# Two MLP projections of a streaming encoder step as seven block products in place of eight

## What is computed

```
h = rmsnorm(x, norm_mlp[i])
x = x + jnp.square(jax.nn.relu(h @ mlp_w_up[i])) @ mlp_w_down[i]
```

## Time and profile before

| | us |
|---|---|
| median of 3 runs | 2936.48 |
| lowest and highest | 2935.74, 2940.26 |
| span of the profiled execution | 2935.5 |
| TensorE busy in that span | 2839.6 |
| DVE, ACT, POOL busy | 1153.9, 946.4, 622.9 |

### The profile page before, as it was taken

The page is one execution under the profiler, slowest core; times in us unless marked ns, Lnnn a source line. Parts: engine busy times, 40 slices in busy tenths (PEclk is TensorE's granted clock), DMA queues, the critical chain, the costliest instruction groups (busy, mean ns, idle before and its releaser), DMA issues. The chain is left out here.

```text
span 2935.5 us, 41843 instructions
## 1 busy us (share of the span) xinstructions
PE 2839.6 (97%) x16003; PEld 2508.1 (85%) x16003; DVE 1153.9 (39%) x1778; ACT 946.4 (32%) x1927; POOL 622.9 (21%) x482
## 2 busy tenths in 40 slices
PE   7989997899999999999899999998999999999998
PEld 6878896788998899889798877776899899989997
DVE  5666663343332233223411008886443233323333
ACT  4344444221221122113222229996132112112212
POOL 3100002021211121112121116664031122112211
PEclk9999999999999999999999999999999999999999
DMA  4211113410111011011134448655021011101111
GB/s 141 84 59 44 43 52 97 156 36 29 58 50 36 29 57 50 23 42 58 65 126 152 146 124 196 148 143 168 1 65 44 29 43 57 43 29 43 57 33 75
DMA packets 190619, 214.97 MB, mean 73 GB/s; under 512 B 17312, under 2 KB 151968, under 8 KB 190496
## 3 DMA queue, kind: packets, MB, share of 16 engines
q1 hardware_dynamic: 190496, 213.30, 24.2%
HBM read 165.65 MB, written 47.61 MB: 73 GB/s over the span
## 5 line engine op out<-in xcount | busy, mean ns | idle before, releaser
L1576 DVE TENSOR_TENSOR x<-m_ps,x 128x512 f32<-128x512 f32 x324 | 223.9, 691 | 606.2 <-PE m_ps L76 606.2
L1621 DVE TENSOR_TENSOR m_sq<-m_relu 128x384 f32<-128x384 f32 x192 | 170.8, 890 | 504.9 <-ACT m_relu L1508 504.9
L1508 ACT ACTIVATE m_relu<-m_ps 128x384 f32<-128x384 f32 x192 | 94.5, 492 | 507.5 <-PE m_ps L76 507.5
L74 PE MATMUL m_ps<-h_h,m_up0h 128*128 128x384 f32 x768 | 257.0, 335 | 0.0
L76 PE MATMUL m_ps<-h_h,m_up0l 128*128 128x384 f32 x768 | 256.7, 334 | 0.0
L75 PE MATMUL m_ps<-h_l,m_up0h 128*128 128x384 f32 x768 | 256.7, 334 | 0.0
L74 PE MATMUL m_ps<-h_h,m_up1h 128*128 128x384 f32 x768 | 256.5, 334 | 0.0
L75 PE MATMUL m_ps<-h_l,m_up1h 128*128 128x384 f32 x768 | 256.5, 334 | 0.0
L76 PE MATMUL m_ps<-h_h,m_up1l 128*128 128x384 f32 x768 | 256.5, 334 | 0.0
L1503 ACT CAST m_dn0h<-m_dn_raw 128x1024 fp32r<-128x1024 f32 x16 | 16.8, 1053 | 546.7 <-PE m_ps L76 546.6
L1556 POOL TENSOR_TENSOR m_dn0l<-m_dn_raw,m_dn0h 128x1024 fp32r<-128x1024 f32 x16 | 38.2, 2390 | 527.7 <-ACT m_dn0h L1503 527.7
(11 more groups left out here) (573 smaller groups left out, 7177.8 us busy)
## 6 DMA issues: line engine op xcount, KB each, us to landing
m_up_raw<-in_mlp_w_up SPq DMA_DIRECT2D x64, 512.0 KB, 4.7
m_dn_raw<-in_mlp_w_down SPq DMA_DIRECT2D x64, 512.0 KB, 3.4
h_raw<-scratch_oT SPq DMA_DIRECT2D x4, 1536.0 KB, 15.2
scratch_qr<-a_qrst SPq DMA_DIRECT2D x9, 512.0 KB, 3.4
a_x<-in_x_prompt SPq DMA_DIRECT2D x8, 512.0 KB, 4.9
b_qr<-scratch_qr SPq DMA_DIRECT2D x4, 1024.0 KB, 6.8
scratch_oT<-b_o SPq DMA_DIRECT2D x32, 128.0 KB, 1.7
x<-in_x_prompt SPq DMA_DIRECT2D x4, 1024.0 KB, 13.6
```

The costliest lines, as they stand in the source:

```text
L74: pe.matmul(out, w[0], m[0], start=start, stop=False)
L1508: act.activation(relu[n % 2][:], up_bank(n, first), ACT.Relu).then_inc(relu_done.sem, 1)
L1576: dve.tensor_tensor(x[:, t, cols], bank[:, 4 + n % 3, :], x[:, t, cols], ALU.add).then_inc(added.sem, 1)
L1621: dve.tensor_tensor(sq[n % 2][:], relu[n % 2][:], relu[n % 2][:], ALU.mult).then_inc(sq_done.sem, 1)
```

## The change

The core of the diff:

```diff
+        tok_slot = dict(A11=0, S2=1, S3=2, S1=3, A12=0, S4=1, A22=2)
+        wt_slot = dict(B11=0, T2=1, T3=2, T1=3, B21=1, B22=2, B12=3)
...
+        NORM_ORDER = (0, 1, 2, 3, 8, 4, 5, 6, 7)
...
+        def down_bank(c, n, hp):
+            return 2 * ((14 * c + PAIR_HALF[n] + hp) % 3)
...
+            for c in range(CHUNKS):
+                more = c + 1 < CHUNKS
+                token_hi(c, "S3")
+                token_hi(c, "A12")
+                weight_hi(c, "B21")
+                token_hi(c, "S4")
+                weight_hi(c, "B22")
+                token_hi(c, "A22")
+                weight_hi(c, "B12")
+                weight_hi(c, "T4")
+                if more:
+                    token_hi(c + 1, "S1")
+                    token_hi(c + 1, "A11")
+                    weight_hi(c + 1, "B11")
+                    token_hi(c + 1, "S2")
+                    weight_hi(c + 1, "T2")
+                    weight_hi(c + 1, "T1")
+                    token_hi(c + 1, "u8")
+                    weight_hi(c + 1, "T3")
...
+                if i >= 2 and final:
+                    act.wait_ge(y_out[i % 2].sem, 16 * (i // 2))
+                elif i >= 2:
+                    act.wait_ge(turned_2.sem, 2 * (i - 1))
...
+            def third_sum(c):
+
+                raw = wt_raw[c % 2]
+                pool.wait_ge(*weight_in(c, "22"))
+                if c:
+                    pool.wait_ge(down.sem, down_at(c - 1, "s1"))
+                else:
+                    pool.wait_ge(prod.sem, 9 * PAIRS_FF)
...
+            for c in range(CHUNKS):
+                fourth_sum(c)
+                weight_lo(c, "B21")
+                if c == CHUNKS - 1:
+                    pool.wait_ge(summed.sem, down_at(c, "P1"))
+                    for hp in range(2):
+                        out = total["P2"][:, 2 * hp:2 * hp + 2, :]
+                        pool.tensor_tensor(out, out, total["P1"][:, 2 * hp:2 * hp + 2, :], ALU.add).then_inc(
+                            join_pool.sem, 1)
...
+                dve.tensor_tensor(out, src, out, ALU.add).then_inc(summed.sem, 1)
...
+                token_sum(c, "S3")
+                token_lo(c, "S3")
+                for hp in range(2):
+                    accumulate(c, "P1", hp)
+                token_lo(c, "A12")
+                for hp in range(2):
+                    accumulate(c, "P6", hp)
+                token_sum(c, "S4")
+                token_lo(c, "S4")
                 if last:
...
+                    join_totals("P6", "P1", [(summed, down_at(c, "P6"))])
+                for hp in range(2):
+                    accumulate(c, "P7", hp)
+                token_lo(c, "A22")
+                if last:
+                    join_totals("P3", "P6", [(join_2, 2)])
+                    join_totals("P7", "P6", [(summed, down_at(c, "P7"))])
+                for hp in range(2):
+                    accumulate(c, "P5", hp)
...
+                    token_sum(c + 1, "S1")
+                for hp in range(2):
+                    accumulate(c, "P2", hp)
+                accumulate_sample(c, 0)
+                if not last:
+                    token_lo(c + 1, "A11")
+                    token_lo(c + 1, "S1")
+                    token_sum(c + 1, "S2")
...
+                    token_lo(c + 1, "S2")
+                    weight_sums(c + 1)
+                    token_lo(c + 1, "u8")
+                    for hp in range(2):
+                        accumulate(c, "P4", hp)
...
+                up_product(p, "P1", alpha, "A11", "B11", True)
...
+                pe.wait_ge(parted.sem, 3 * p + 1)
+                up_product(p, "P6", alpha, "S2", "T2", False)
+                after(pe, joined, 3 * (p - 2) + 3)
+                up_product(p, "P5", delta, "S1", "T1", True)
+                pe.wait_ge(parted.sem, 3 * p + 2)
...
+                up_sample(p, 0)
+                up_sample(p, 1)
...
+                pe.wait_ge(parted.sem, 3 * p + 3)
+                up_product(p, "P4", alpha, "A22", "T4", False)
+                pe.wait_ge(joined.sem, 3 * p + 2)
+                up_product(p, "P3", delta, "S4", "B22", False)
...
+                after(pe, summed, down_emptied(c, n, hp))
+                pe.wait_ge(tok_lo[a].sem, c + 1)
+                pe.wait_ge(wt_lo[b].sem, c + 1)
+                for i in range(2):
+                    t = 2 * hp + i
+                    for j in range(2):
+                        last = product(pe, bank[:, down_bank(c, n, hp) + i, :],
+                                       [u[:, j, t * P:(t + 1) * P] for u in tok_op[a]],
+                                       [w[:, j, :] for w in wt_op[b]], j == 0, j == 1)
...
+                for n, a, b in (("P1", "A11", "B11"), ("P6", "S2", "T2"), ("P7", "S3", "T3"), ("P5", "S1", "T1"),
+                                ("P2", "A12", "B21")):
+                    for hp in range(2):
+                        down_product(c, n, hp, a, b)
+                down_sample(c, 0)
+                for hp in range(2):
+                    down_product(c, "P3", hp, "S4", "B22")
+                down_sample(c, 1)
+                down_product(c, "P4", 0, "A22", "T4")
+                if last_chunk and not final:
+                    next_turn(0)
+                    next_turn(1)
+                down_product(c, "P4", 1, "A22", "T4")
```

More of the change, by code:

```diff
@@ new lines, in output_and_mlp_stage @@
+        w_o_parts = made + [parts for parts, _ in w_o_t[len(made):]]
+        w_o_raw = loaded + [raw[:] for _, raw in w_o_t[len(loaded):]]
+        gain = place("gain", [P, D_MODEL], r_at)
+        xn = [place(f"xn{u}", [P, D_MODEL], r_at + 4 * KIB * (u + 1)) for u in range(2)]
+        sum_2 = place("sum2", [P, QUARTER, P], r_at + 12 * KIB)
+        stat = place("stat", [P, NT, 3], r_at + 34 * KIB)
+        stat_2 = place("stat2", [P, NT, 3], r_at + 34 * KIB + 128)
+        half = place("half", [P, 1], r_at + 34 * KIB + 256)
@@ L1361, in output_and_mlp_stage @@
-        added = signal("add", 3)
-        def chunks(engine, body):
-            body(0, False, True)
-            with engine.Fori(1, CHUNKS - 1) as c:
-                body(c, False, False)
-            body(CHUNKS - 1, True, False)
-        def up_bank(n, first):
-            return bank[:, (7, 4)[n] if first and n < 2 else (n + 2) % 4, 0:GROUP]
+        out_done, added = signal("out"), signal("add")
+        x_out = [signal(f"xout{t}") for t in range(NT)]
+        squared, mean, rs, normed, turned, half_set = (signal(n) for n in ("sq", "mean", "rs", "xn", "xt", "half"))
@@ new lines, in up_product @@
+            def up_product(p, kind, out, a, b, start):
+                pe.wait_ge(up_lo.sem, up_at(a, p))
+                if b in ("T2", "T3", "T4"):
+                    out = out.rearrange("p (q c) -> p q c", c=P)
+                for k in range(4):
+                    last = product(pe, out, [w[:, k, :] for w in up[a]], [features(b, k, s) for s in range(2)],
+                                   start and k == 0, k == 3,
+                                   not start)
+                last.then_inc(prod.sem, 1)
@@ new lines, in up_sample @@
+            def up_sample(p, j):
+                out = up_banks(p)[3][:, j * P:(j + 1) * P]
+                for i, n in enumerate((("A11", "A12"), ("A21", "A22"))[j]):
+                    pe.wait_ge(up_lo.sem, up_at(n, p))
+                    for k in range(4):
+                        last = product(pe, out, [w[:, k, :] for w in up[n]], [y[:, 4 * i + k, :] for y in h8],
+                                       i == 0 and k == 0, i == 1 and k == 3)
+                last.then_inc(prod.sem, 1)
@@ L1701, in sb_operands @@
+            if not final:
+                for i in range(2, NT):
+                    next_turn(i)
+    return [piece[:] for piece in ahead]
 def sb_operands(nc, ctx, name):
```

1161 lines of the change are left out of this document (850 added, 311 removed).

## The result

| | before | after |
|---|---|---|
| median, us | 2936.11 | 3003.11 |
| lowest and highest of 4 runs | 2934.92, 2940.26 | 2999.34, 3004.56 |
| span of the profiled execution | 2935.5 | 3002.5 |
| ratio, with 95% interval | | 1.0224, 1.021 to 1.0239 |

What follows compares the result with a forecast made beforehand. The prediction took TensorE, busy 97% of the span, to bound the kernel before. Up -18, up's starts +4, down +51 and tails +23 made +60 on 2935.5, so 2996 us, 2965 to 3030 for the forecast itself, 2885 to 3040 overall.

Steps and rivals of the forecast that it cites:

- the walk: Down part: the four engine queues followed in order with DVE/POOL turns, giving a steady chunk of 50.1 us, bound by DVE.
- Up, TensorE: Up part: 128-column matmuls at 0.111 us make pairs of 24.4 us, 780 us in place of 798, -18 us.
- the line down to 0.067: Up's short matmuls at 0.067 us, extrapolated from wider ones: rival of 68 us less, 2928 us, 16%.
- Up, the start: First up pair of each layer: the last tile's sums and splits stand between, +2 us a layer.
- Down, steady chunk: Down chunks between first and last: 50.1 us, TensorE waiting in the second halves of P1, P6 and P5.
- third stall: Steady down chunk: P5's second half starts at 25.6 us, not 19.0, after DVE's first add of P7.
- DVE's PSUM adds, priced at 1.22: Down part: each 1024-column DVE add from PSUM takes 1.22 us and is free of turns with POOL.
- First chunk: First down chunk of a layer: T2 and S3 come later, P5's second half 7 us later, 57.1 us.
- Last chunk: Last down chunk of a layer: ten joins of totals on DVE in place of eight operand steps, 59.5 us.
- Tails: Norms after the last down matmul: layer 1 +15 us with two store buffers, layer 0 +8, together +23 us.
- The rival of the falling clock: Down part: after stalls the granted clock falls, one more product per chunk at half speed, 43 us, 3040 us; 11%.
- The rival of DVE keeping up: Down part: DVE stands under 8.7 us per chunk, TensorE sets 43.5 us chunks, 2865 us; 20%.

Runs made afterwards that it cites:

- run 12: Changed kernel with the 48 short sample-row matmuls per up pair streaming 256 columns in place of 128 (sample results wrong): 3012.5 us, 1.0256.
- run 1: Changed kernel with ACT casting u8 ahead of T2, T1 and T3 at each change of chunk: 2954.64 us, 1.0059.
- run 5: Changed kernel with four of POOL's low parts (B11, T2, B21, T4) cut to 64 of 512 columns from chunk 1 on: 2980.44 us, 1.0146.
- run 3: Changed kernel with twelve filler matmuls of 512 columns ahead of P1's second half in chunks 1 to 7: 3000.63 us, 1.0221.
- run 2: Changed kernel with DVE adding P4's two halves ahead of u8's low part, ACT's order kept: 3023.54 us, 1.0296.
- run 4: Changed kernel with four store buffers in place of two in the last norm of layer 1: 2995.2 us, 1.02.
- run 7: Run 6 with four store buffers in the last norm of layer 1: 2934.04 us, 0.999.
- run 6: Run 1 with DVE adding P1's first half between S3's sum and its low part: 2943.42 us, 1.002.
- run 9: Run 7 with DVE adding P7's first half between S4's sum and its low part: 2923.33 us, 0.9952.
- run 11: Run 9 plus P4's join on POOL, last-chunk DVE joins halved between adds, and POOL's first two inverse norms ahead of its joins: 2914.3 us, 0.9926.

## Why the prediction was right, and where it was not

The sign and the size held, 2996 forecast and 3003 measured, and so did the mechanism: DVE, held up by ACT's order of casts and by turns with POOL, keeps the PSUM banks from TensorE. Part of how close the number came is luck, as one step of the walk failed and two terms that were mis-sized offset each other. The terms, both layers together, from the starts of TensorE's first and last matmul of each part:

| term | predicted | measured |
|---|---|---|
| up, both layers | -14 | -8 |
| down, both layers | +51 | +49 |
| tails | +23 | +25 |
| start of up | 0 | +1 |
| sum | +60 | +67 |

Up takes 396.7 us in layer 0 (632.65 to 1029.37) and 396.9 in layer 1, against 400.6 before. Down takes 418.0 and 415.0 against 392; the prediction had 417.2. The tail of layer 1 is 25.7 us in place of 8.4. In layer 0 the next stage's first matmul starts 24.7 us after the last down product, not 10.8, which is +13.9, less the turns of 6.3 us that stood among the down products before.

- **Up, TensorE: right.** Pairs come exactly 24.46 us apart and TensorE is never idle past the first. The 48 short matmuls take (24.46 - 84 x 0.2267) / 48 = 0.113 us each, and start 0.112 apart (725.98 to 727.32 for twelve), where 0.111 was taken from the earlier trace rows; the line down to 0.067 is out, and run 12 says so again. The estimate of 107 ns from the Trainium skill, "TensorE: Matmul & The Clock Gate", section on LDWEIGHTS, agrees within 6 ns; the 81 ns of its section on the back-to-back gap do not hold for these fp32r products.
- **Up, the start: mis-sized.** Up takes 5.3 us a layer more than its 16 pairs (396.7 less 16 x 24.46). The kernel before had 1.0 of that in its first chunk too, so the term of +2 us a layer was 4.3. TensorE waits 2.49 us for A12's low part at 638.02, the granted clock is 0.70 in the 4 us from 636 on, and one turn (0.8 us) is left in the path. Twice 2.3 us is two thirds of the 7 us missed.
- **Down, steady chunk: 50.1 forecast, 48.7 and 49.0 measured; one step of the walk failed.** The stall before P1's second half was to end at 5.5 and ended at 6.0, for the reason given (the cast of u8 behind T2 and T1, and the turn with POOL); runs 1 and 5 show both parts. The step that failed is "POOL has T3's low part to 6.6 and takes T1's to 9.0, so DVE's sum S3 ends at 10.1". DVE and POOL asked within 0.01 us of each other, and at 12 of 14 changes of chunk DVE went first: S3's sum ended at 8.2. So of the 3.5 us of waiting that the walk had before P6's second half at most 1.0 was left, where the clock stayed up, and mostly nothing behind slow matmuls; its third stall never came. The walk had no slow matmuls (1.6 us a chunk), and by run 3 that is no error in the sum. In the one steady chunk where POOL did go first the length was 50.86 us, and run 2 has S3 in second place each time and chunks of 50.5: the walk's own case.
- **DVE's PSUM adds, priced at 1.22,** take 1.21 alone but follow each other by 1.13 us. None of the 212 of 128x1024 goes over 1.23 us, whatever POOL does, while low parts and sums take up to 3.44. That rule of the trace held.
- **First chunk: 57.1 forecast, 58.2 measured, but not by the walk given.** TensorE stands 2.0 us in P1, 4.8 for T2's low part from POOL before P6 and 2.9 in P6, and not before P5's second half. **Last chunk: 59.5 forecast, 67.4 and 62.8 measured.** The joins were mis-sized: of the five pairs of halves three take 6.6 or 6.7, 4.6 and 4.5 us under POOL's turns, where they had been counted like operand steps, 2 x 1.22, and TensorE stands 7.65 us (5.40 in layer 1) behind the first. Down's total came out within 2 us of 417 because the steady chunks gave 8 and 7 us and the last ones took 8 and 3 back. That is luck.
- **Tails: right within 2 us,** by the reason given, two buffers and a store between uses (runs 4 and 7). Layer 1 was to take 23.5 us and took 25.7. The first square stood 11 us before TensorE's end, and DVE's adds of P3 and of the sample rows still came before the first scale (2972.03).
- **The rival of the falling clock** was half true: it fell at 12 of the 14 changes of chunk, and cost nothing but where it lasted longest (run 3). Its ground was misread: the eight transposes of the earlier trace rows have no wait before them, and their starts are 0.109 us apart as in the earlier trace rows. **The rival of DVE keeping up** was closer than its place suggested: three lines in other places (runs 1, 6 and 9) make down run at 43.5 us a chunk.
- **Slips in the sums,** none of which moves the forecast by more than 1 us: DVE's work in a chunk adds up to 35.0, not 34.8, and 2 x 25.2 is 50, not 51. The window of the earlier trace rows from 636 to 1427 is not the eight chunks, which run from 631.6 to 1430.5 with transposes among them, but a chunk does take 98.9. Half way from 2996 to the first rival's 2865 is 2930; 2900 is half way from the kernel before.

So the seven products save what they should, 88 us of down products and, after the sample rows, 16 of up. Against these 104 us stand 64 in the steady chunks over the 43.5 us of their products, 43 in the last chunks with the joins, 29 in the first ones, 25 in the tails, where the norm lay under products before, and 9 at the starts of up. Runs 1, 6 and 9, the order of three small operations, give back 70 us. With them, four store buffers and the joins in halves (run 11), the change is a gain of 0.74%. No run changed the first chunks or the starts of up, so what they could give stays open.

## What to carry to other kernels

When a change brings a busy engine down to the pace of another, look for the one instruction on which the other stands, and ask for every queue whether something that is ready waits behind something that is not: the cast of u8 could run when s1's matmuls ended, near 1179.5, and ran at 1187.39. Where two engines take turns, the walk through the queues gave the stall to within a microsecond up to the first tie; from a tie on keep both outcomes, since here it fell both ways in one run. A faster or busier TensorE is worth nothing where its next wait is for the same chain (runs 3 and 11), so count the time from the chain that ends last.

## What the runs showed of the hardware

- **Turns.** A DVE operation with all inputs in SBUF and a POOL operation exclude each other; the one that waits is delayed by what is left of the other, so 0.68 becomes 1.50 and 1.21 becomes 3.4. The Trainium skill, "SBUF — State Buffer", section on who interferes with whom, states the exclusion; that they alternate, and that a tie within 0.01 us went to DVE 12 times and to POOL twice in the changed kernel, only these traces show.
- **Clock.** After 12 of 14 stalls of 3.14 us TensorE's granted clock fell to 0.50 (1.2 GHz), in nine for some 3 us and in three for some 6 (1239.21, 1385.97, 2771.66); in some chunks at once (1190.72), in others about 1.4 us after work had begun again (1095.0). After the two others (2625.86, 2871.24) it stayed at 1.00. It also stayed there after the stalls of 2.33 us (run 5), 1.63 (run 1) and 1.00 (run 3) in the steady chunks, but near the 2.49 us at 638.02 it fell. In run 3, with 2.7 us of matmuls in the place of the stall, it stayed at 1.00. So the length of a stall alone does not tell whether it falls.
- **Short matmuls.** fp32r products start 0.227, 0.120 and 0.112 us apart for 512, 256 and 128 columns: from 256 down the cost hardly falls.
